# Starting a two-block transformer kernel with the query projection instead of the memory projection, on inputs turned on the host

## The reference, cut to what matters

```
def rms_norm(x, g):
    y = x * lax.rsqrt(jnp.mean(x * x, axis=-1, keepdims=True) + 1e-6)
    return y * g
...
h = rms_norm(x, attn_norm_g)
qa, ka, va, qb, kb, vb, f_logit, g_logit = split(h @ w_in)      # 1024 x 5128
...
km, vm = jnp.split(mem_n @ w_kv, 2, axis=-1)                    # mem_n = rms-normed memory, w_kv 1024 x 512
```

## Time and profile before

| | |
|---|---|
| device time, 3 runs | 742.03 us median (741.42 to 743.98) |
| profiled execution: device time, span | 742.64 us, 740.8 us |
| PE busy | 728.6 us (98%), 3772 instructions |
| DVE busy | 507.3 us (68%) |
| ACT busy | 481.4 us (65%) |
| DMA | 128.61 MB, 174 GB/s on average |
| first matmul of a projection | 9.79 us after the start of the span |

### The profile page before, as it was taken

One profiled execution on the slowest core, in us unless ns is written; L12 is line 12 of the kernel. 1 busy time (PEld: TensorE's weight loads), 2 busy tenths in 40 slices (PEclk: granted clock), 3 DMA queues, 4 the chain that ended last, 5 costly groups with the idle time before them and its releaser, 6 DMA issues.

```text
span 740.8 us, 10577 instructions
## 1 busy us (share of the span) xinstructions
PE 728.6 (98%) x3772; PEld 603.2 (81%) x3772; DVE 507.3 (68%) x779; ACT 481.4 (65%) x764; POOL 8.4 (1%) x18
## 2 busy tenths in 40 slices
PE   8999999999999999999999999999899999999998
PEld 5888897887788888888888888877688888888886
DVE  5775787676767788677455658999787765567540
ACT  6875677875358788777434887677847776557420
POOL 0003000000000000000000000000000000000000
PEclk9999999999999999999999999999999999999999
DMA  8784845435556664546664544411266755566630
GB/s 327 251 269 120 245 135 164 137 128 162 167 166 207 226 226 155 181 132 231 225 199 144 185 128 138 162 30 58 81 203 214 234 185 165 171 224 224 205 110 28
DMA packets 70460, 128.61 MB, mean 174 GB/s; under 512 B 4915, under 2 KB 17044, under 8 KB 70420
## 3 DMA queue, kind: packets, MB, share of 16 engines
q1 hardware_dynamic: 69684, 125.62, 52.8%
q10 hardware_dynamic: 736, 2.46, 1.1%
HBM read 127.02 MB, written 1.05 MB: 173 GB/s over the span
## 4 chain that ended last, share of the span: by engine, by line
PE 91%; ACT 3%; DVE 2%; DMA 2%; issue 1%; SPq 0%; ACTq 0%; DVEq 0%
PE acc L601 27%; PE acc L603 27%; PE acc L602 26%; PE banks L741 1%; DVE b_wlo L1577 1%; PE banks L623 1%; PE banks L636 1%; PE banks L919 1%; DMA b_gates<-in_mem 1%; DMA b_raw<-in_w_in 1%; ACT b_whi L1080 1%; DMA b_raw<-in_w_ffn_up 1%; PE banks L653 1%; PE banks L668 1%; PE banks L782 1%
## 5 line engine op out<-in xcount | busy, mean ns | idle before, releaser
L1577 DVE TENSOR_TENSOR b_wlo<-b_raw,b_whi 128x1024 fp32r<-128x1024 f32 (+4 forms) x232 | 267.9, 1187 | 89.4 <-ACT b_whi L1080 88.9
L1080 ACT ACTIVATE b_whi<-b_raw 128x1024 fp32r<-128x1024 f32 (+4 forms) x232 | 232.4, 1029 | 93.2 <-PE acc L603 35.8
L601 PE MATMUL acc<-b_whi,b_hhi 128*128 128x512 f32 (+4 forms) x512 | 198.4, 388 | 0.7 <-DVE b_hlo L1886 0.6
L603 PE MATMUL acc<-b_wlo,b_hhi 128*128 128x512 f32 (+4 forms) x512 | 193.8, 378 | 0.0
L602 PE MATMUL acc<-b_whi,b_hlo 128*128 128x512 f32 (+4 forms) x512 | 193.5, 378 | 0.0
L601 PEld LDWEIGHTS acc<-b_whi,b_hhi 128*128 128x128 f32 x512 | 96.3, 188 | 19.0 <-issue 2.3
L603 PEld LDWEIGHTS acc<-b_wlo,b_hhi 128*128 128x128 f32 x512 | 96.3, 188 | 16.1
L602 PEld LDWEIGHTS acc<-b_whi,b_hlo 128*128 128x128 f32 x512 | 96.5, 188 | 14.5
L601 PE MATMUL acc<-b_whi,b_ohi 128*128 128x512 f32 x256 | 102.8, 402 | 0.0
L603 PE MATMUL acc<-b_wlo,b_ohi 128*128 128x512 f32 x256 | 100.5, 393 | 0.0
L602 PE MATMUL acc<-b_whi,b_olo 128*128 128x512 f32 x256 | 100.3, 392 | 0.0
(11 more groups left out here) (265 smaller groups left out, 744.3 us busy)
## 6 DMA issues: line engine op xcount, KB each, us to landing
b_raw<-in_w_in SPq DMA_DIRECT2D x48, 512.0 KB, 4.4
b_raw<-in_w_ffn_up SPq DMA_DIRECT2D x40, 512.0 KB, 4.8
b_raw<-in_w_ffn_in SPq DMA_DIRECT2D x40, 512.0 KB, 4.6
b_raw<-in_w_ffn_down SPq DMA_DIRECT2D x22, 512.0 KB, 5.5
b_raw<-in_w_ffn_out SPq DMA_DIRECT2D x22, 512.0 KB, 4.1
b_raw<-in_w_out SPq DMA_DIRECT2D x16, 512.0 KB, 3.8
b_raw<-in_w_in SPq DMA_DIRECT2D x12, 412.0 KB, 4.9
b_raw<-in_w_in SPq DMA_DIRECT2D x8, 410.0 KB, 3.9
```

Source lines behind the costliest of these rows:

```text
L601: nc.tensor.matmul(o, a, wh, start=first, stop=False)
L603: mm = nc.tensor.matmul(o, a, wl, start=False, stop=last)
L1080: ins = A(whi[:, n % SPLIT, 0:c["nk"], 0:c["n"]], raw[:, n % RAW, 0:c["nk"], 0:c["n"]], ACT.Copy)
L1577: ins = V.tensor_tensor(wlo[:, n % SPLIT, 0:c["nk"], 0:c["n"]], raw[:, n % RAW, 0:c["nk"], 0:c["n"]], whi[:, n % SPLIT, 0:c["nk"], 0:c["n" ...
```

## The change

1. The host passes `x` and the memory also transposed (`xT`, `memT`, 1024 x 256), all short vectors laid out as columns (`cols`, 128 x 110), and the gains of the heads inside `consts`. The untransposed `x` and memory are still loaded, for the residual and for the squares of the norms.
2. `in_hi` and `in_lo` make the operand parts from the transposed input, one 128-row tile at a time, with the norm's gain as a per-partition scale. The 32 transposes of the norm turns of `mem` and `x1`, `norm_gain` for `x1`, `gcol` and the `vectors` transpose are gone; `idle(2)` stands alone at the start.
3. The first projection is `qa`. Its four chunks go by `by_rows`: the loads, `hi`, `lo` and matmuls proceed in steps of 128 rows (6 matmuls for each row tile: the three passes, each for both token tiles).
4. `mkv` runs after `va` and before `qb`. All lists of the first block are written anew; those of the second are unchanged.

The new parts, and the lists up to where they run in step again:

```diff
+            def by_rows(name, c):
+                g = groups[name]
+                hi, lo = lhs_of[g["lhs"]]
+                for k in range(CK * c, CK * c + CK):
+                    weights = (slice(None), c, k % CK, slice(0, g["n"]))
+                    first, last = k == 0, k == g["kt"] - 1
+                    pe.wait_ge(*at("in hi", f"{TURNED[name]} {k}"))
+                    pe.wait_ge(sem("hi ready" if k % CK else "first hi"), c + 1)
+                    for t in range(T):
+                        nc.tensor.matmul(acc[0][t][:, 0:g["n"]], hi[:, k, t * P:(t + 1) * P], whi[weights],
+                                         start=first, stop=False)
+                    pe.wait_ge(*at("in lo", f"{TURNED[name]} {k}"))
...
+                    pe.wait_ge(sem("lo ready" if k % CK else "first lo"), c + 1)
...
+            def in_hi(which, k):
+                if (which, k) == ("x1", 0):
+                    act.wait_ge(sem("columns in"), 16)
+                act.wait_ge(sem(f"{which}T {piece_of(k)} in"), 16)
+                done(A(SIDE[which][0][:, k, :], turned_in(which, k), ACT.Copy, scale=norm_column(which, k)),
+                     "in hi", f"{which} {k}")
+            def in_lo(which, k):
+                dve.wait_ge(*at("in hi", f"{which} {k}"))
+                hi, lo = SIDE[which]
+                done(V.scalar_tensor_tensor(lo[:, k, :], turned_in(which, k), norm_column(which, k),
+                                            hi[:, k, :].bitcast(F32), ALU.mult, ALU.subtract), "in lo", f"{which} {k}")
...
+            turned("x1", 0)
             for n, c in enumerate(chunks):
+                if 0 < n < RAW:
+                    turned("x1", n + 1)
+                elif n < RAW + T:
+                    if n >= RAW:
+                        tokens(x, "x", "x", n - RAW)
+                elif n == RAW + T:
+                    sp.dma_start(cst[:, :], dram["consts"]).then_inc(sem("consts in"), 16)
+                elif n < RAW + T + 1 + len(PIECES):
+                    turned("mem", n - RAW - T - 1)
+                elif n < RAW + T + 1 + len(PIECES) + T:
+                    tokens(memx, "mem_2", "mem", n - RAW - T - 1 - len(PIECES))
...
-            idle(1)
-            pe.wait_ge(sem("identity in"), 16)
-            gain_column()
-            idle(1)
+            idle(2)
...
+ORDER1["pe"] = [("gemm", "qa", 0), ("gemm", "qa", 1), ("gemm", "qa", 2), ("gemm", "qa", 3), ("gemm", "ka", 0),
+     ("gemm", "ka", 1, 0), ("gemm", "va", 0, 0), ("gemm", "ka", 2, 0), ("gemm", "ka", 3, 0), ("gemm", "va", 0, 1),
+     ("gemm", "ka", 1, 1), ("gemm", "va", 1, 0), ("gemm", "va", 2, 0), ("gemm", "ka", 2, 1), ("gemm", "ka", 3, 1),
+     ("gemm", "va", 3, 0), ("gemm", "va", 1, 1), ("gemm", "va", 2, 1), ("gemm", "va", 3, 1), ("gemm", "mkv", 1),
+     ("gemm", "mkv", 3), ("gemm", "qb", 0, 0), ("gemm", "qb", 1, 0), ("gemm", "mkv", 0), ("gemm", "mkv", 2),
+     ("gemm", "qb", 0, 1), ("gemm", "qb", 1, 1), ("gemm", "qb", 2), ("gemm", "qb", 3, 0), ("turn", "qa"),
+     ("turn", "mk"), ("gemm", "fg0", 0, 0), ("turn", "ka"), ("gemm", "fg0", 0, 1), ("scores", 0),
...
+ORDER1["act"] = [("in hi", "x1", 0), ("first hi", "qa", 0), ("in hi", "x1", 1), ("hi", "qa", 0), ("in hi", "x1", 2),
+     ("first hi", "qa", 1), ("in hi", "x1", 3), ("hi", "qa", 1), ("in hi", "x1", 4), ("first hi", "qa", 2),
+     ("in hi", "x1", 5), ("hi", "qa", 2), ("in hi", "x1", 6), ("first hi", "qa", 3), ("hi", "ka", 0),
+     ("norm squares", "x1", 0), ("in hi", "x1", 7), ("norm squares", "x1", 1), ("norm guess", "x1"), ("hi", "ka", 1),
+     ("sums", "qa", 0, 1), ("hi", "ka", 2), ("hi", "va", 2), ("hi", "qa", 3), ("in hi", "mem", 0, 1),
+     ("in hi", "mem", 2, 3), ("hi", "mkv", 0), ("in hi", "mem", 4, 5), ("in hi", "mem", 6, 7),
...
+     ("guess", "ka"), ("sums", "va", 1), ("hi", "mkv", 2), ("hi", "mkv", 3), ("sums", "mkv", 0, 1), ("guess", "mk"),
+     ("hi", "fg0", 2), ("turn", "mk"), ("turn", "qa"), ("turn", "ka"), ("hi", "kb", 0), ("sums", "qb", 0),
...
+ORDER1["dve"] = [("in lo", "x1", 0), ("first lo", "qa", 0), ("in lo", "x1", 1), ("lo", "qa", 0), ("in lo", "x1", 2),
...
+     ("in lo", "x1", 5), ("lo", "qa", 2), ("in lo", "x1", 6), ("first lo", "qa", 3), ("lo", "ka", 0),
+     ("in lo", "x1", 7), ("norm root", "x1"), ("lo", "qa", 3), ("lo", "va", 3), ("squares", "qa"), ("lo", "mkv", 0),
+     ("in lo", "mem", 0, 1), ("in lo", "mem", 2, 3), ("in lo", "mem", 4, 5), ("in lo", "mem", 6, 7), ("lo", "mkv", 3),
+     ("lo", "mkv", 1), ("norm root", "mem"), ("lo", "qb", 2), ("heads", "qa"), ("squares", "ka"), ("lo", "fg0", 1),
+     ("heads", "ka"), ("squares", "mk"), ("heads", "mk"), ("lo", "kb", 0), ("scores", 0), ("lo", "fg1", 1),
+     ("scores", 1), ("divide", 0), ("squares", "qb"), ("divide", 1), ("heads", "qb"), ("sums", "fg0"),
...
```

More of the change, by code:

```diff
@@ L143 @@
-ORDER1["act"] = [("hi", "mkv", 0), ("norm hi", "mem", 0, 0), ("hi", "mkv", 1), ("norm hi", "mem", 0, 1),
-     ("norm hi", "mem", 1, 0), ("hi", "mkv", 3), ("norm hi", "mem", 1, 1), ("norm squares", "mem", 0),
-     ("norm squares", "mem", 1), ("norm guess", "mem"), ("hi", "qa", 0), ("norm hi", "x1", 0, 0, 1), ("hi", "qa", 1),
[11 rows of a table removed]
-     ("gate log", "fg2"), ("mix", 0), ("pv", 3), ("sums", "vb", 1), ("scores", 5), ("hi", "bra1", 0), ("probs", 4),
-     ("mix", 1), ("next gain", "x1"), ("mix", 2), ("scores", 6), ("pv", 4), ("hi", "bra0", 0), ("probs", 5),
[7 rows of a table removed]
@@ new lines @@
+ORDER1["act"] = [("in hi", "x1", 0), ("first hi", "qa", 0), ("in hi", "x1", 1), ("hi", "qa", 0), ("in hi", "x1", 2),
[5 rows of a table added]
+     ("norm squares", "mem", 0), ("sums", "ka", 0, 1), ("hi", "mkv", 1), ("norm squares", "mem", 1),
+     ("norm guess", "mem"), ("hi", "qb", 1), ("sums", "va", 0), ("guess", "qa"), ("hi", "fg0", 1), ("hi", "fg0", 0),
+     ("guess", "ka"), ("sums", "va", 1), ("hi", "mkv", 2), ("hi", "mkv", 3), ("sums", "mkv", 0, 1), ("guess", "mk"),
[6 rows of a table added]
+     ("mix", 0), ("probs", 3), ("hi", "vb", 3), ("scores", 4), ("gate log", "fg2"), ("pv", 3), ("sums", "vb", 1),
+     ("sums", "vb", 0), ("scores", 5), ("hi", "bra1", 0), ("probs", 4), ("scores", 6), ("pv", 4), ("hi", "bra0", 0),
+     ("probs", 5), ("pv", 5), ("mix", 1), ("gate log", "fg3"), ("scores", 7), ("mix", 2), ("next gain", "x1"),
[6 rows of a table added]
@@ L812, in ffn2 @@
                         chunk("d2_1", c, t)
-            def gain_column():
-                pe.wait_ge(sem("mem gain row in"), 16)
-                nc.tensor.transpose(acc[1][0][:, 0:KT], memg, ident[0:KT, 0:KT]).then_inc(sem("mem gain turned"), 1)
             def idle(n):
@@ L1016, in _ @@
                 for g in range(len(FG) - 1):
-                    if n == groups[f"fg{g}"]["first"]:
+                    if n == groups[f"fg{g}"]["last"]:
                         if g == 0:
-                            for bank in range(2 * T):
-                                sp.wait_ge(*at(f"bank{bank} full", "memT"))
+                            sp.wait_ge(*at("in lo", "mem 7"))
                             sp.wait_ge(*at("squares", "mem 1"))
@@ L1376, in _ @@
                     hi_to(groups[n]["at"][rest[0]])
+                elif kind == "first hi":
+                    first_hi(groups[n]["at"][rest[0]])
+                elif kind == "in hi":
+                    for k in rest:
+                        in_hi(n, k)
                 elif kind[:4] == "norm":
@@ L1891, in _ @@
                     lo_to(groups[n]["at"][rest[0]])
+                elif kind == "first lo":
+                    first_lo(groups[n]["at"][rest[0]])
+                elif kind == "in lo":
+                    for k in rest:
+                        in_lo(n, k)
                 elif kind[:4] == "norm":
```

285 lines of the change are left out of this document (129 added, 156 removed), and 61 rows, old and new, of the table pick.

## The result

The changed kernel takes **751.9 us** (median of 4 runs, 749.9 to 753.7), beside 743.0 us for the kernel before on the same chip: ratio 1.0114, 95% interval 1.0088 to 1.0140. It is slower by 1.1%; 738.7 us and a chance of 0.07 for "slower" had been given. Its profiled execution took 749.9 us (span 748.1), 7.3 us more than that of the kernel before.

What follows compares the result with a forecast made beforehand. PE, busy 98%, bounds the kernel; 2.3 us from the start plus 1.0 from `probs 0` take the profiled 742.6 to 739.3, the median 0.6 lower at 738.7 us. Range 735.0 to 741.6, likeliest case 737.0 to 739.9.

Steps and rivals of the forecast that it cites:

- First matmul: Start of the first projection: PE begins at about 5.5 us, 4.3 us before the old one.
- chunk 4: First weight chunk of `ka`, loaded behind `qa`, `xT` and one tile of `x`: lands at 15.2 us.
- the wait at row tile 7: Last row tile of `qa`: PE waits about 3 us because ACT's `in hi` stands behind `hi ka 0` and squares.
- the waits of 1.4 and 0.5 us: PE waits of 1.4 us after `ka 0` and 0.5 us after `ka 1` and `va 0`, for splits of later chunks.
- the first half of `ka 3`: PE ends this half chunk at 29.4 us, or 29.7 if the clock falls behind the wait at row tile 7.
- The 2.3 us of gain: First 30 us: what is left of the earlier start and shed PE work after waits, including the `vectors` transpose.
- The step that failed first: From 29.4 us to the turn of `qa`: ACT three chunks ahead, PE no longer waiting, so the 2.3 us stay.
- The part on the bounds: Uncertainty of the start: 1.5 to 3 us of gain; 1.5 MB more DMA spread over the first 35 us.
- the rival with the turn of `mk`: Turn of `mk` ahead of `fg0` holds PE and makes the kernel slower; slack 1.3 us, chance 0.07.
- The two rivals: Apparently slower by the turn of `mk` (0.07), and nothing measurable, late loads among its reasons (0.27); the text names neither pair.
- the rest of the block: Re-ordered remainder of the first block: stalls too few for any list to win much, nothing booked.
- The 1.0 from `probs 0`: First block: PE's 1.4 us stall on `divide 0` goes as that moves behind `scores 1`; gain 1.0, bounds 0 and 1.0.

Runs made afterwards that it cites:

- e13: Changed kernel with 224 unused bytes ahead of the activation's two buffers; one profiled execution, 747.8 us.
- e2: Changed kernel with PE's turn of `mk` just ahead of `scores 0` and ACT's part behind its part of the turn of `ka`; median 750.1 us, ratio 1.0091.
- e10: Changed kernel, 96 bytes of padding behind `b_cst`, memory's tokens loaded ahead of chunks 15 and 16, their norm steps moved along; median 748.6 us, ratio 1.0069.
- e11: e10 with the order of e2 and the lists of e4, 96 bytes of padding behind `b_cst`; median 743.7 us, ratio 1.0008.
- e3: Changed kernel without the loads of the memory's tokens, its norm squares reading `x` instead; median 747.3 us, ratio 1.0050.
- e4: Changed kernel with the three lists of the kernel before behind `scores 0` in the first block; median 748.4 us, ratio 1.0059.
- e7: Kernel before with one unused buffer of 32 bytes behind `b_cst` and nothing of the change; median 746.0 us, ratio 1.0028.
- e12: Changed kernel with 480 unused bytes ahead of the activation's two buffers, giving them their addresses in the kernel before; median 747.2 us, ratio 1.0055.
- e14: e10 with the order of e2 and the lists of e4, but 480 bytes of padding behind `b_cst`; median 741.25 us, ratio 0.9968.

## Why the prediction was wrong

**Right, nearly to the tenth: the first 30 us.** First matmul at 4.88 (said 5.5); chunk 4 landed at 15.9 (15.2); the wait at row tile 7 was 2.65 us (about 3), for the reason given; behind it the clock fell, and this cost nothing, for the waits of 1.4 and 0.5 us that the sum had next did not appear. In e13, where the clock stayed at 1.00 behind the same wait, they did: 1.21 and 0.54 us. (e2, e10 and e11 kept it too and had 1.2 us at the same place.) Either way the first half of `ka 3` ended at 29.6 and 29.8 (said 29.4 or 29.7). The 2.3 us of gain were there. The Trainium skill ("TensorE: Matmul & The Clock Gate", part 1) has an idle stretch lower the clock; of the eleven traces with this wait at tile 7 (2.40 to 2.75 us) seven agree (the kernel after: 2.65 us, then 0.50), and four kept full clock, one of them behind 2.75.

**The step that failed first: "from there ACT is three chunks ahead again; I followed the lists up to the turn of `qa` and found PE no longer waiting".** ACT was not ahead, because the landings were not followed beyond chunk 4. The part on the bounds spread "the 1.5 MB more of DMA over the first 35 us, beside the lookahead of four chunks", but between 22 and 40 us 2 MB for the memory stand in SP's order among the weights. ACT, in order, waited for weights 1.8, 1.7 and 1.5 us, came late with `sums ka` (43.6 to 46.0, asked for at 43.1) and the splits behind it, and PE lost 2.85 us (e3 and e10 take them away).

**The second: the rival with the turn of `mk` was undersized.** It had a slack of 1.3 us. Its place and its engine were right. PE came to it at 67.2 (said 64.7; the 2.85 of the step above more than account for the difference), but the heads of `mk` were done at 69.1, not 63.4: DVE did three `lo` until 61.8 and the heads of `ka` until 65.0, both fed by what ACT had late, and those of `mk` only then. The loss is 2.0 us, of which e2 shows 1.2 to be had. The two rivals, priced apart, have one cause.

**The third: "the rest of the block is re-ordered as well, but its stalls are so few that no list can win much, and I book nothing".** Nothing to win is not nothing to lose. The pause before `ffn1` grew by 1.7 us; e4 shows that this is the lists. At 255.9 another 1.1 came, which stayed with the old lists (e4), so its cause stays open.

**The fourth had no term at all: where the buffers lie.** The diff changes the length of `b_cst` and drops `vec` and `gcol`; the prediction speaks only of the work that goes with them. It costs 3.5 us by the pitch, the largest single term (e7, e12, e13).

The sum: 739.3 was said of the profiled execution. 2.85 + 2.0 + 1.7 + 1.1 + 3.5 = 11.15 more, less the 1.3 won between 524 and 553 us, is 749.15; measured 749.9. The 1.0 from `probs 0` arrived: 3.0 late at the turn of `ka` and 1.9 late behind it, and no wait there. But the new place of `divide 0` was not needed for it, and the size is in part luck: in e4, e11 and e14 `divide 0` stands behind `lo fg2 0` as in the kernel before, and there is no wait either (0.04 us). In e14 ACT waited 1.0 us for a chunk at 78.5 us, in the kernel before 2.0 at 79.6, and DVE came to `divide 0` 0.75 earlier.

## What to carry to other kernels

A stream of loads with a fixed lookahead has to be followed to the end of the stretch in which bytes were added, chunk by chunk, together with what the in-order engine does while it waits; the first late chunk is not the last one. When an edit changes the size of any buffer, compare the start addresses of all operand buffers behind it, and look at the step between weight loads in stretches that the edit doesn't touch: a slower pitch shows neither in waits nor in busy time. And a gain behind which stands a list fitted to the old times is kept only if that list's next due times are checked too.

## What the runs showed of the hardware

- The place of a matmul's weights in the partition changes its pitch at full clock from 0.2267 to 0.2333 us (2.9%), in all sixteen kernels by the remainder of the start by 256 bytes: 128 good (0.2267), 160 and 192 bad (0.2333), 0 at 0.2324. ACT's and DVE's instructions on the moved buffers kept their durations (`b_alo` from `b_y` and `b_ahi`, 128x1024: 1226 ns before, 1225 after). The Trainium skill ("SBUF — State Buffer", "Operand start alignment") says that an operand must start at a multiple of its element size, and that this is about legality, not speed; for speed these runs show that more is needed.
- The same pause doesn't always bring the clock down: behind 2.04 us at 524 us it fell in the profile of before and stayed at 1.00 in e7 (it fell in seven of the sixteen traces, though the pause is 2.04 us in each); behind 2.65 and 2.62 us at 18 us it fell in the kernel after and stayed in e13. Each fall takes 1.7 us of clock, by the sum of what the windows lack of 1.00 (0.03, 0.50 and 0.32 of 2 us each at 18 to 24 us). How much of that arrives depends on what PE would have waited for: 0.9 us at 524 us (before against e7), nothing at 18 us.
